# State-space heads: a third place for sums and exponentials, VectorE's products two heads behind, inputs and scores in one bank

## The reference, cut to what matters

```
scores[s,t]   = B_group[s,:] . C_group[t,:]
M[d][s,t]     = exp(a(t) - a(s)) * scores[s,t]      (s <= t forwards, s >= t backwards, else 0)
y[h,t]        = sum over d of ( sum over s of M[d][s,t] * dt(s) x[h,s]  +  exp(a(t)) * C_group[t,:] . h0[d][h] )
y             = (y + D * x) * silu(z),   z = x_in @ W_z
out           = rms_norm(y) @ W_out
```

## Time and profile before

| | |
|---|---|
| median of 3 runs | 2171.96 us (2171.58 to 2174.76) |
| the profiled execution, its own time | 2168.83 us |
| its span in the trace | 2167.1 us |
| mean granted TensorE clock | 0.961 |
| PE, DVE, ACT, POOL busy | 91%, 52%, 46%, 59% |
| heads stage in the trace | about 1422.7 to 1557 us, projection to 1609.8 us |

### The profile page before, as it was taken

The page is one execution under the profiler, slowest core; times in us unless marked ns, Lnnn a source line. Parts: engine busy times, 40 slices in busy tenths (PEclk is TensorE's granted clock), DMA queues, the critical chain, the costliest instruction groups (busy, mean ns, idle before and its releaser), DMA issues.

```text
span 2167.1 us, 34254 instructions
## 1 busy us (share of the span) xinstructions
PE 1961.5 (91%) x13757; PEld 1736.7 (80%) x13757; DVE 1122.0 (52%) x1489; ACT 1005.2 (46%) x1694; POOL 1268.1 (59%) x588
## 2 busy tenths in 40 slices
PE   6889989999899989989999889998879997978997
PEld 6878788888799966868888878876669986947996
DVE  7773247770200074137776565678755632845641
ACT  4454434443344463434544344468734545424542
POOL 9737556669688702646559434400377985415985
PEclk9999999999899999999999999999999998988999
DMA  6325256674455503356675222311234543314543
GB/s 248 139 93 194 98 221 267 269 268 178 158 192 187 185 19 134 120 218 243 264 283 180 79 78 78 117 59 59 78 127 175 188 181 117 136 58 146 191 178 116
DMA packets 48320, 342.29 MB, mean 158 GB/s; under 512 B 5264, under 2 KB 6288, under 8 KB 7248
## 3 DMA queue, kind: packets, MB, share of 16 engines
q1 hardware_dynamic: 45968, 328.22, 41.4%
q0 software_dynamic: 2240, 12.49, 1.5%
HBM read 339.65 MB, written 1.05 MB: 157 GB/s over the span
## 4 chain that ended last, share of the span: by engine, by line
PE 60%; DVE 21%; ACT 8%; DMA 4%; issue 3%; POOL 3%; DVEq 0%; SPq 0%; ACTq 0%; POOLq 0%
PE bank L1653 12%; PE bank L1599 9%; PE bank L1603 9%; PE bank L1601 9%; DMA ring<-slabs_dram 4%; DVE arena L853 2%; PE bank L1697 2%; POOL w_lo L2079 2%; PE bank L1203 2%; PE bank L1205 2%; PE bank L1206 2%; PE bank L1634 2%; PE bank L1633 2%; PE bank L1631 2%; ACT arena L1057 2%
## 5 line engine op out<-in xcount | busy, mean ns | idle before, releaser
L2079 POOL TENSOR_TENSOR w_lo<-ring,w_hi 128x1024 fp32r<-128x1024 f32 x360 | 880.7, 2469 | 322.7 <-ACT w_hi L2586 322.5
L1599 PE MATMUL bank<-x_hi,w_hi 128*128 128x256 f32 x2176 | 618.7, 284 | 30.5 <-POOL w_lo L2079 16.9
L1603 PE MATMUL bank<-x_lo,w_hi 128*128 128x256 f32 x2176 | 620.8, 285 | 0.0
L2586 ACT ACTIVATE w_hi<-ring 128x1024 fp32r<-128x1024 f32 x448 | 448.7, 1052 | 283.8 <-DMA ring<-slabs_dram 283.8
L1599 PEld LDWEIGHTS bank<-x_hi,w_hi 128*128 128x128 f32 x2176 | 416.6, 191 | 52.4 <-issue 44.8
L1603 PEld LDWEIGHTS bank<-x_lo,w_hi 128*128 128x128 f32 x2176 | 416.0, 191 | 0.0
L1601 PE MATMUL bank<-x_hi,w_lo 128*128 128x256 f32 x1472 | 412.9, 281 | 0.0
L2524 ACT ACTIVATE arena<-bank 128x512 f32<-128x512 f32 (+1 forms) x274 | 142.6, 535 | 354.8 <-PE bank L1603 248.1
L2079 POOL TENSOR_TENSOR w_hi<-ring,w_hi 128x1024 fp32r<-128x1024 f32 x88 | 217.5, 2493 | 137.9 <-ACT w_hi L2586 137.9
L1601 PEld LDWEIGHTS bank<-x_hi,w_lo 128*128 128x128 f32 x1472 | 280.9, 191 | 0.0
L1601 PE MATMUL bank<-x_hi,w_hi 128*128 128x256 f32 x704 | 200.5, 285 | 0.0
(11 more groups left out here) (332 smaller groups left out, 3679.4 us busy)
## 6 DMA issues: line engine op xcount, KB each, us to landing
ring<-slabs_dram SPq DMA_DIRECT2D x312, 1024.0 KB, 4.8
lnrow<-ln_dram POOLq DMA_DIRECT2D x6, 1024.0 KB, 5.1
xt<-xT_dram SPq DMA_DIRECT2D x1, 1024.0 KB, 5.8
xt<-memT_dram POOLq DMA_DIRECT2D x1, 1024.0 KB, 13.5
x<-x_dram POOLq DMA_DIRECT2D x1, 1024.0 KB, 17.4
arena<-ctx_dram POOLq DMA_DIRECT2D x1, 1024.0 KB, 8.8
lnrow<-ln_dram POOLq DMA_DIRECT2D x2, 512.0 KB, 4.6
res<-x POOLq DMA_DIRECT2D x2, 512.0 KB, 2.9
```

Source lines behind the costliest of these rows:

```text
L1599: ins = pe.matmul(dst, wh[:, k, c], src[0][:, k, :], start=(k == 0), stop=False)
L1603: ins = pe.matmul(dst, wh[:, k, c], src[1][:, k, :], start=False, stop=(k == KC - 1))
L2079: pool.tensor_tensor(dst[:, c], ring[:, s, c], w_hi[:, s, c].bitcast(F32), ALU.subtract).then_inc(S["lo_ready"], 1)
L2586: a.activation(w_hi[:, g % RING, c], ring[:, g % RING, c], ACT.Copy) \
```

## The change

Heads q, q+1 and q+2 now have three places: banks 0, 1 and 6, three `seg` and three `ea`. The third `seg` lies in unused columns of `tri`, the third `ea` over values that are no longer needed. VectorE runs head(q-2) behind bounded(q), instead of head(q-1). Bank 6 is no longer free for tokens_of, whose transposes move to bank 2, in turn with the scores: tokens_of(g), inputs_of(g), scores_of(g), masked_scores(g). The group's work moves to other places in each engine's loop: TensorE issues scores_of(g) at j = 0 of group g itself, tokens_of(g+1) at j = 2, and two_heads at even q from 4 on for heads q-4 and q-3, with one more two_heads behind the loop. ScalarE does across_scores(g), gate_of(g-1) and turned(g-2) all at j = 0. VectorE does masked_scores(g) and split_y(g-2) at j = 1, combine(g-1) and inputs_of(g+1) at j = 3. No engine gets or loses an instruction.

```diff
-        seg = cut(22528, 2, 768)
+        seg = [cut(22528, 2, 384), cut(23296, 2, 384),
+               tri[:, 0:2, :, :].rearrange("p a b c -> p a (b c)")[:, :, P:512]]
+        sum_bank = (0, 1, 6)
...
-        ea = [dist[:, i, :].rearrange("p (d t) -> p d t", d=2) for i in range(2)]
+        ea = [dist[:, i, :].rearrange("p (d t) -> p d t", d=2) for i in range(2)] \
+            + [cut(27136, 2, 512)[:, :, 0:T]]
...
             def inputs_of(g):
...
-                v.wait_ge(full["dve"][6], L.filled(6))
+                v.wait_ge(full["dve"][2], L.filled(2))
...
-                        bank[6][:, :].rearrange("p (t h e) -> p t h e", t=NT, h=4), w, ALU.mult)
+                        bank[2][:, :].rearrange("p (t h e) -> p t h e", t=NT, h=4), w, ALU.mult)
...
-                ins.then_inc(free["dve"][6], 1)
-                v.wait_ge(free["dve"][6], L.freed(6))
+                ins.then_inc(free["dve"][2], 1)
+                v.wait_ge(free["dve"][2], L.freed(2))
...
             def bounded(q):
...
-                b = q % 2
+                b = sum_bank[q % 3]
...
-                v.tensor_tensor(seg[:, b, :].rearrange("p (d a c) -> p d a c", d=2, a=3)[:, :, 0:3:2, :],
+                v.tensor_tensor(seg[q % 3].rearrange("p d (a c) -> p d a c", a=3)[:, :, 0:3:2, :],
...
-                step(v.tensor_tensor(cea[q % 4], ea[q % 2],
+                step(v.tensor_tensor(cea[q % 4], ea[q % 3],
...
-                v.wait_ge(free["act"][q % 2], marks["heads_act"][q % 2] + q // 2 + 1)
-                v.tensor_tensor(mT[q % 4], seg[:, q % 2, :], gT[:, g % 2, :], ALU.mult) \
+                b = sum_bank[q % 3]
+                v.wait_ge(free["act"][b], marks["heads_act"][b] + q // 3 + 1)
+                v.tensor_tensor(mT[q % 4].rearrange("p (d c) -> p d c", d=2), seg[q % 3],
+                                gT[:, g % 2, :].rearrange("p (d c) -> p d c", d=2), ALU.mult) \
...
-            for q in range(SH + 5):
+            for q in range(SH + 6):
                 g, j = q // 4, q % 4
                 if q < SH:
                     bounded(q)
-                if 1 <= q <= SH:
-                    head(q - 1)
-                if j == 0 and g >= 2:
+                if 2 <= q < SH + 2:
+                    head(q - 2)
+                if j == 1 and 1 <= g < SG:
+                    masked_scores(g)
+                if j == 1 and g >= 2:
                     split_y(g - 2)
-                if j == 2:
+                if j == 3:
                     if g >= 1:
                         combine(g - 1)
                     if g + 1 < SG:
                         inputs_of(g + 1)
-                if j == 3 and g + 1 < SG:
-                    masked_scores(g + 1)
...
             def decays(q):
...
-                b = q % 2
+                b = sum_bank[q % 3]
...
-                if q >= 2:
-                    a.wait_ge(S["m_ready"], q - 1)
-                a.activation(ea[b], bank[b][:, :].rearrange("p (d t) -> p d t", d=2), ACT.Exp) \
+                if q >= 3:
+                    a.wait_ge(S["m_ready"], q - 2)
+                a.activation(ea[q % 3], bank[b][:, :].rearrange("p (d t) -> p d t", d=2), ACT.Exp) \
...
-                for n, (d, st, at) in enumerate([(0, 0, 0), (0, 1, 256), (1, 0, 384), (1, 1, 640),
-                                                 (0, 0, 128), (1, 1, 512)]):
-                    part = seg[:, b, at:at + P]
+                for n, (d, st, at) in enumerate([(0, 0, 0), (0, 1, 256), (1, 0, 0), (1, 1, 256),
+                                                 (0, 0, 128), (1, 1, 128)]):
+                    part = seg[q % 3][:, d, at:at + P]
...
-            for q in range(SH + 4):
+            for q in range(SH + 5):
                 g, j = q // 4, q % 4
                 if q < SH:
                     decays(q)
-                if j == 3 and g + 1 < SG:
-                    across_scores(g + 1)
-                if j == 0 and g >= 1:
+                if j == 0 and 1 <= g < SG:
+                    across_scores(g)
+                if j == 0 and 1 <= g <= SG:
                     gate_of(g - 1)
-                if j == 3 and g >= 1:
-                    turned(g - 1)
+                if j == 0 and g >= 2:
+                    turned(g - 2)
...
             def sums(q):
...
-                b = q % 2
+                b = sum_bank[q % 3]
...
             def tokens_of(g):
...
-                pe.wait_ge(free_of(6), frees(6))
+                pe.wait_ge(free_of(2), frees(2))
...
-                        ins = pe.transpose(bank[6][:, tt * T + c * P:tt * T + (c + 1) * P],
+                        ins = pe.transpose(bank[2][:, tt * T + c * P:tt * T + (c + 1) * P],
...
-                fill(ins, 6, "dve")
+                fill(ins, 2, "dve")
...
                 g, j = q // 4, q % 4
...
                 gate_part(g, j)
-                if j == 1 and g + 1 < SG:
+                if j == 2 and g + 1 < SG:
                     tokens_of(g + 1)
-                if j == 2 and g + 1 < SG:
-                    scores_of(g + 1)
-                if q % 2 and q >= 3:
-                    two_heads((q - 3) // 2)
+                if j == 0 and g:
+                    scores_of(g)
+                if q % 2 == 0 and q >= 4:
+                    two_heads((q - 4) // 2)
+            two_heads(SH // 2 - 2)
```

## The result

| | before | after |
|---|---|---|
| median, 20 runs each | 2167.48 us (2164.58 to 2178.39) | 2175.11 us (2168.86 to 2184.7) |
| span of the profiled execution | 2167.1 us | 2172.2 us |
| inputs_of(0) starts | 1423.45 | 1427.71 |
| from there to the projection's slab 1, below "the stage" | 143.16 | 145.71 |
| from slab 1 to the end | 600.5 | 598.8 |

The ratio is 1.0029, 95% interval 1.0017 to 1.0042: the change makes the kernel slower, by 6.3 us (3.7 to 9.1).

A forecast was written before the change was run, and what follows sets the result against it. Engines' mutual waits were taken as the bound, then the ring through shared bank 2. Start -1.3, six groups -3.8, end 0, four low stretches +6.8, end's clock +0.8: +2.5 us, 2174.5 us; range 2166.9 to 2179.5.

The forecast's parts named there:

- no clear difference: Whole kernel: change within about 0.2%, 4.3 us, what a measurement can tell from no change; chance 0.54.
- What bounded before, and that the lag would end it: Heads stage, 17.08 us a group: engines' waits for one another bound it; third place and two-head lag remove them.
- The sign that ScalarE's wait before `ea` would be nearly gone: Table of waits: ScalarE's wait before `ea` for VectorE's minimum, 23.6 us in 15 waits, nearly gone.
- The ring: Each group: inputs_of empties bank 2, then scores, two_heads, sums, minimum; period 16.45 us, gain 0.63 in each of six groups.
- The clock: Groups 2 to 7: clock falls behind TensorE's 2.1 us idle before scores, 1.7 us each; four of six, +6.8 us.
- The rate of the seven idle times elsewhere in the trace: Earlier trace: behind six of seven TensorE idle times of 2.0 to 2.4 us the clock fell to 1.2 GHz.
- The rule of the Trainium skill: First rival, TensorE in groups 2 to 7: clock stays up or falls once or twice, 2166.9 up to 2171 us; chance 0.18.
- The start: Before minimum(4): first minimum 1.6 us later, then no extras ahead of minimum(3); net gain 1.3 us.
- The end, priced at nothing: minimum(28) to hi_swo(1): about 20 us as before, with 1.65 us of hold-up by lo_swo(0); 0 us at full clock.
- TensorE's 0.8 us behind GpSimd: Stage end: a clock fall brings TensorE to slab 1 about 1 us behind GpSimd; +0.8 us, chance three in four.

The follow-up runs named there:

- the three profiles with this order: Profiles of the changed kernel, of it once more unchanged, and of it with lo_swo(0) moved behind add_squares(6) on GpSimd; stages 145.71, 147.40 and 152.41 us.
- the filler: Changed kernel with the first gate quarter of groups 2 to 7 computed twice on TensorE, ahead of its idle time; ratio 0.9988 to before, stage 141.25 us.
- The second profile of after: The changed kernel profiled once more, nothing changed; stage 147.40 us, two of six periods long.
- the shared bank in the old order: Kernel before with only tokens and inputs put through bank 2, nothing moved, two places, lag of one head; ratio 1.0113, 24 us slower.
- the four kernels with the scores behind the sums: Changed kernel with scores_of(g) behind sums(4g+1), alone 0.9976; plus split_y later 0.9968, or turned earlier 0.9958; the latter plus first tokens in bank 6 0.9943.

## Why the prediction was right, and where not

The median of the changed kernel, 2175.11 us, lies in the range and 0.6 from the forecast, but that nearness is luck. The forecast stood on a base of 2171.96 us, and before measured 4.5 us less over 20 runs. The change was worth +6.3 us (3.7 to 9.1), and I forecast +2.5, which is below that interval. I gave no clear difference 0.54 and slower 0.28; slower it is, by a small amount.

- *What bounded before, and that the lag would end it*: right for VectorE, whose waits for exponentials are gone; the fall from 17.08 goes no further than the ring through the shared bank. The sign that ScalarE's wait before `ea` would be nearly gone did not come: 24.2 us, was 23.6. Which of the third place, the lag and the new order ended VectorE's waits no run tells apart.
- *The ring*: 16.45 forecast, 16.55 measured; VectorE's wait 1.45 forecast, 1.59 measured; TensorE's idle 2.1 forecast, 2.09 measured. Moving the scores took the wait away and shortened the periods, so the mechanism is shown.
- *The clock*: right in kind, both terms off. I took four falls of six; the three profiles with this order have two each (and one of the three one more at the start). The rate of the seven idle times elsewhere in the trace, six, did not carry over. A fall costs 2.23 us, not 1.7: 1.64 of clock, and 0.59 because VectorE, late, meets add_squares.
- *The rule of the Trainium skill*, "TensorE: Matmul & The Clock Gate", section "Why this matters for your kernels": by it the clock would have stayed up behind an idle time this short. In the three profiles it stayed up behind 12 of the 18 idle times of 2.09 us and fell behind 6; the filler shows what the falls are worth.
- *The start*: -1.3 forecast, -1.44 measured.
- *The end, priced at nothing*: **this step failed.** I gave lo_swo(0) 1.65 us of hold-up, as `cea` has in the earlier trace rows (2.39 less 0.69 is 1.70). It was 3.3 us, since VectorE, no longer waiting itself, ran into both pieces, and add_squares(6) added 1.0. Before, part of that hold-up had fallen into a wait of VectorE for `ea`. From minimum(28) to hi_swo(1) 20.0 forecast, 22.75 measured, 19.4 with the pieces moved away. TensorE's 0.8 us behind GpSimd did not come: it still waited 0.26 for slab 1.

The sum by measured terms is -1.44 - 3.18 + 4.46 + 2.70 = +2.55, where I had -1.3 - 3.8 + 6.8 + 0.8 = +2.5: too many falls made up for an end that was too cheap, which is luck as well. The second profile of after has +4.2 inside the stage. The ratio's +6.3 is higher than both, its lower bound 3.7 between them; whether unprofiled executions have more falls, or whether what lies around the stage adds to it, stays open. The mean clocks of the runs don't decide it: 0.956 for after, 0.957 to 0.959 for the kernels whose profiles show periods without a fall. The filler's 9 us (3 to 14) against 4.5 in the stage points the same way and settles no more.

## What to carry to other kernels

When two streams are put into one buffer, look at what is queued behind the one that now waits: here moving one call by one place in one engine's order, with not an instruction more or less, turned +0.3% into -0.2%, and with two more such moves, one of a bank, into -0.6%. Count idle time of TensorE twice, once as the wait and once as the clock behind it: here one in three idle times of 2.09 us cost 1.64 us more by the clock. And when a wait of VectorE is removed, ask which GpSimd instruction it will now run into.

## What I had not expected of the hardware

- Behind idle times of 2.09 us with the same work before and after them the clock fell in six of eighteen (three profiles, six groups each); behind the 4.3 us of the shared bank in the old order it fell in all six periods; behind the 0.3 to 1.0 us of the four kernels with the scores behind the sums in no period at all (six each). At the start, behind 1.61 us, it fell in one profile of seven.
- Useless matmuls made the kernel faster: 10 us of them took 4.5 us off the stage of the changed kernel, and 9 (3 to 14) off its time by the two ratios.
- GpSimd's sums and VectorE's products of two SBUF tensors don't share, they take turns: add_squares (1.27 us) that starts first makes `cea` 1.28 instead of 0.69, one that starts behind `mT` takes 1.71 or 2.06 itself and `mT` stays at 0.96. Beside VectorE's instructions that read PSUM neither changes (masked scores 0.88 us beside add_squares and apart from it). So 0.6 us a group hang on which of the two starts first. The Trainium skill, "SBUF — State Buffer", section "SBUF: two separate sides", calls this an exclusive lock for whoever starts first; these durations agree with it.
- The stretches ahead of the stage and behind it (slab 1 to the end, 598.6 to 603.4 us) move by up to 13 and 5 us from one profile to the next in kernels that are the same there (inputs_of(0) between 1423.45 and 1436.52 us), while the stage without falls repeats within 0.1.
